# Where the first norm's row vectors live, and where a unit's position row is computed: a two-layer decoder trunk on one core

## The chip, the core and the metric

The kernel runs on one core of a Trainium2 chip (trn2). The metric is the device time of one execution in microseconds (us); the smaller the better. Engines are named as the profile names them: PE is TensorE's matmul, PEld its weight load, DVE is VectorE, ACT is ScalarE, POOL is GpSimd, SP is SyncE, which here issues nearly all DMAs.

## The reference, cut to what matters

Two layers. Each has three token mixers, an output projection with a layer norm, and a mixture of 16 experts with a second layer norm. The change lies in the first norm's last step and in the experts.

```python
def grouped_moe(x, router_w, router_b, w_gate, w_up, w_down):
    ...
    for e in range(N_EXPERTS):
        he = jax.nn.silu(h @ w_gate[e]) * (h @ w_up[e])
        out = out + gate[:, e:e + 1] * (he @ w_down[e])
    ...

for l in range(DEPTH):
    ...
    x = layer_norm(DEEPNORM_ALPHA * x + heads_out @ w_out[l], ln1_g[l], ln1_b[l])
    ffn = grouped_moe(x, router_w, router_b, exp_w_gate[l], exp_w_up[l], exp_w_down[l])
    x = layer_norm(DEEPNORM_ALPHA * x + ffn, ln2_g[l], ln2_b[l])
```

256 tokens of 1,024 values; an expert is 512 wide; every token goes to 2 of 16 experts. The output is the whole `x`, float32.

## The kernel before, in words

**Mixers, then experts, twice.** PE runs through a layer in a written order: projection, mixers, output projection (L1396), transposes of the normalized rows, router, then the experts. Everything from the routing on is in `experts_t` (PE), `experts_s` (ACT) and `experts_v` (DVE), each called through `two_ways`: the engine waits for `v_flag`, loads the word `crowded` and branches. With these inputs the way with `rounds == 1` is taken: one unit of 64 slots for each expert, so 16 units (N = 16).

**Weights.** SP issues all weight loads in one fixed order, 1 MB each: for an expert two halves of gate and of up, then two of down, 6 MB. They go into a ring of 8 + 6 slots (`ring`, `ring_more`) plus two that serve once a layer. A load waits until the last matmul that reads its slot's former content has counted (`last_use`: t_wgu for gate and up, t_wd for down). So 16 MB of a layer's 96 MB of expert weights can be there before the first unit, and from then on a load starts as PE gives a slot back.

**The entry to the experts, in order.** DVE computes the selection, `pick` (a 0/1 matrix that gathers a unit's tokens), the flag and the gates. PE gathers the first four blocks of 128 channels for the first eight experts (`gather`, L427), ACT copies each into `xg` with the norm's gain and shift per channel (L696, s_first), PE runs `first_half` (L518: the first half of expert 0's gate and up), takes the branch, gathers blocks 4 to 7, waits for v_pick, runs `slot_gates(0)` (L532) and two transposes of the positions (L631), and then waits for all eight counts of s_first. Only then comes `hidden(0, 1)` (L552), the second half of expert 0's gate and up. DVE, before its branch, runs `rows_of_x1` (L1581, L1582): `x_tm` times `ln1_g`, plus `ln1_b`, for two tiles of 128 tokens, four operations of 128x1024. The rows of `ln1_g` and `ln1_b`, the same in all 128 partitions, lie in `x_cm`, which is read until the router is done; POOL therefore loads them (two DMAs of 512 KB, L992) only once v_sel has counted. v_pick is given by DVE behind its branch.

**A unit n.** PE: `hidden(n, 1)`, `scatter(n-1)` (L603: y of the unit before, as y_hi + y_lo, added to the tokens' rows in banks 0 to 3 through `pick_t`), `turn(n)` (L567, four transposes of `gu`, waits for v_gu), `position_row(n)` (L611, four matmuls of 32x128 that spread the expert's row of slot numbers), `hidden(n+1, 0)`, `down(n)` (L586). Unit 0 has `hidden(1, 0)` ahead of `turn(0)`. DVE: `take_hidden` (L772: `gu`, the hidden row times the gate), `turned_pick` (L795: `pick_t` from the position row), `product` (L779), `y_low` (L787). ACT: `silu` (L712), `y_high` (L718). The hidden rows of unit n are in bank 4 or 5 (`b_hid[n % 2]`), and the position row overwrites them there once `gu` is taken; `turn` uses bank 6, `down` and the gates bank 7 (`b_y`).

```python
            for n in range(N):
                ...
                if n < N - 1:
                    turn(n)
                    position_row(n)
                ...
                if 0 < n < N - 1 and not turn_of_group:
                    hidden(n + 1, 0)
```

## Time and profile before

| | |
|---|---|
| time, three runs | 864.36, 864.50, 866.28 us; median 864.5 |
| the profiled execution | 866.47 us, its span 864.6 us |
| PE | 800.7 us busy, 93% of the span |
| DVE, ACT, POOL | 315.2 us (36%), 180.6 us (21%), 26.0 us (3%) |
| DMA | 245.87 MB, mean 284 GB/s |
| granted clock of PE, mean | 0.973 |

The time of an execution is a little more than the span from its first to its last instruction. A group of matmuls is given with its start, its length and, in brackets, what PE waited for before it. PE counts as busy also where it runs at half clock. The DMA share is that of the core's 16 DMA engines; it can read slightly over 1.

### The profile page before, as it was taken

Reading aid. Unit: us, or ns where it says so; the run is one execution under the profiler, and the core shown is the slowest. Engines: PE = TensorE matmul, PEld = TensorE weight load, DVE = VectorE, ACT = ScalarE, POOL = GpSimd, SP = SyncE. Lnnn points to the kernel's source line nnn. Section 1 sums busy time; section 2 is a strip of 40 time slices with the busy share of each in tenths; the row PEclk is TensorE's granted clock in tenths of the full one; section 3 lists DMA queues with packets and bytes.
Section 4 is the critical chain, followed back from the end, with each engine's and each line's share of the span. In section 5 each row is a group of like instructions: output and inputs, shape, how many; then the busy total and the mean of one; then the engine's idle time right before and its main releaser. Section 6 shows DMA issues by size and latency. Waiting matters only on the chain. (4 is left out here: it accounts for less than half of the span.)

```text
span 864.6 us, 13075 instructions
## 1 busy us (share of the span) xinstructions
PE 800.7 (93%) x5493; PEld 436.2 (50%) x5493; DVE 315.2 (36%) x646; ACT 180.6 (21%) x371; POOL 26.0 (3%) x103
## 2 busy tenths in 40 slices
PE   9999999988999999989799999999799999999883
PEld 8888666545333333323288876664453333333331
DVE  1296445565111111111343964373741111111115
ACT  1142322333001110000222223232330011100001
POOL 7100000000000000000000000000000000000000
PEclk9999999998999999999989999999999999999998
DMA  9945200397899999999945532014969999999992
GB/s 281 322 150 181 99 2 2 134 425 267 303 417 420 421 421 419 422 422 420 398 143 190 186 108 99 2 68 161 423 255 346 423 420 421 420 421 423 420 421 98
DMA packets 55252, 245.87 MB, mean 284 GB/s; under 512 B 8356, under 2 KB 13328, under 8 KB 30608
## 3 DMA queue, kind: packets, MB, share of 16 engines
q1 hardware_dynamic: 53840, 240.20, 70.3%
q0 software_dynamic: 1344, 4.72, 1.7%
q8 instruction: 48, 0.79, 0.4%
q14 instruction: 20, 0.16, 0.1%
HBM read 243.85 MB, written 1.05 MB: 283 GB/s over the span
## 5 line engine op out<-in xcount | busy, mean ns | idle before, releaser
L552 PE MATMUL bank<-ring,xg 128*64 128x512 f32 x544 | 127.0, 610 | 6.3 <-DMA ring<-in_exp_w_up 3.9
L1054 PE MATMUL bank<-x_cm,ring 128*128 128x256 f32 x576 | 127.8, 383 | 0.9 <-ACT x_cm L2020 0.9
L1054 PEld LDWEIGHTS bank<-x_cm,ring 128*128 128x128 f32 x576 | 110.3, 192 | 17.4 <-ACT x_cm L2020 1.2
L552 PE MATMUL bank<-ring_more,xg 128*64 128x512 f32 x416 | 96.4, 605 | 5.7 <-DMA ring_more<-in_exp_w_up 5.7
L787 DVE TENSOR_TENSOR y_lo<-bank,y_hi 128x512 fp32r<-128x512 f32 x32 | 22.1, 692 | 196.4 <-ACT y_hi L718 187.4
L552 PEld LDWEIGHTS bank<-ring,xg 128*64 128x64 f32 x544 | 38.7, 139 | 76.2 <-issue 74.0
L772 DVE TENSOR_SCALAR x_cm<-bank,g_col 128x512 f32<-128x512 f32 x32 | 24.0, 751 | 107.6 <-PE bank L552 105.1
L552 PEld LDWEIGHTS bank<-ring_more,xg 128*64 128x64 f32 x416 | 30.4, 138 | 58.8 <-issue 57.7
L586 PE MATMUL bank<-ring_more,x_cm 128*64 128x512 f32 x256 | 58.2, 596 | 1.9 <-issue 1.9
L586 PE MATMUL bank<-ring,x_cm 128*64 128x512 f32 x256 | 57.8, 594 | 1.1 <-DVE g_col L763 1.1
L1061 PE MATMUL bank<-ring,x_cm 128*128 128x512 f32 x128 | 57.7, 599 | 0.0
L1396 PE MATMUL bank<-ring,x_cm 128*128 128x512 f32 x128 | 55.6, 592 | 0.0
L718 ACT ACTIVATE y_hi<-bank 128x512 fp32r<-128x512 f32 x32 | 19.1, 597 | 169.8 <-PE bank L586 169.8
L712 ACT ACTIVATE x_cm<-bank 128x256 f32<-128x256 f32 x32 | 12.3, 383 | 179.5 <-PE bank L567 179.5
L1396 PEld LDWEIGHTS bank<-ring,x_cm 128*128 128x128 f32 x128 | 24.0, 190 | 28.7 <-issue 28.7
L1061 PEld LDWEIGHTS bank<-ring,x_cm 128*128 128x128 f32 x128 | 23.7, 190 | 27.3 <-issue 26.8
L586 PEld LDWEIGHTS bank<-ring,x_cm 128*64 128x64 f32 x256 | 18.0, 137 | 35.8 <-issue 34.3
L586 PEld LDWEIGHTS bank<-ring_more,x_cm 128*64 128x64 f32 x256 | 17.9, 137 | 34.0 <-issue 33.3
L696 ACT ACTIVATE xg<-bank,ln_cm 128x512 f32<-128x512 f32 x32 | 23.7, 776 | 46.8 <-PE bank L427 46.1
L567 PE MATMUL bank<-ident,x_cm 128*128 128x128 f32 x128 | 23.9, 309 | 8.6 <-DVE x_cm L772 8.6
L567 PEld LDWEIGHTS bank<-ident,x_cm 128*128 128x128 f32 x128 | 17.9, 209 | 24.1 <-DVE x_cm L772 22.5
L795 DVE TENSOR_SCALAR pick_t<-bank,slot_col 128x128 fp32r<-128x128 f32 x32 | 11.2, 351 | 39.5 <-PE bank L611 37.3
(381 smaller groups left out, 873.9 us busy)
## 6 DMA issues: line engine op xcount, KB each, us to landing
ring<-in_exp_w_gate SPq DMA_DIRECT2D x36, 1024.0 KB, 17.1
ring<-in_exp_w_up SPq DMA_DIRECT2D x36, 1024.0 KB, 18.8
ring_more<-in_exp_w_down SPq DMA_DIRECT2D x32, 1024.0 KB, 18.3
ring<-in_exp_w_down SPq DMA_DIRECT2D x32, 1024.0 KB, 15.4
ring_more<-in_exp_w_gate SPq DMA_DIRECT2D x26, 1024.0 KB, 17.2
ring_more<-in_exp_w_up SPq DMA_DIRECT2D x26, 1024.0 KB, 18.9
ring<-in_w_in SPq DMA_DIRECT2D x24, 1024.0 KB, 8.1
ring<-in_w_out SPq DMA_DIRECT2D x8, 1024.0 KB, 6.3
```

Source lines behind the costliest of these rows:

```text
L552: m = T.matmul(b[half_of(n, i), :], xg[g][:, 4 * h + k, cols], w[:, k, :], start=(h == 0 and k == 0), stop=(h == 1 and k == 3))
L567: m = T.transpose(b_turn[:, tile_(fb)], gu[:, fb::FB], ident[:])
L586: m = T.matmul(b[SL * hf:SL * hf + SL, :], he[n % 2][:, fb, :], w[:, 2 * (fb % 2) + hf, :], start=(fb == 0), stop=(fb == FB - 1))
L696: return A.activation(out_.rearrange("p (u j s) -> p j u s", u=GU, j=TT), in_.rearrange("p (j u s) -> p j u s", u=GU, j=TT), ACT.Identity, ...
L712: mark(A.activation(act_g, b_turn[:].rearrange("p (b a s) -> p b a s", b=FB, a=2)[:, :, side_of(n, 0)], ACT.Silu), "s_silu")
L718: mark(A.activation(y_hi[:], y_bank(n, N)[:], ACT.Copy), "s_yhi")
L772: mark(V.tensor_scalar(gu, b_hid[n % 2][:], g_col[:, n // GU % 2, n % GU:n % GU + 1], None, ALU.mult), "v_gu")
L787: mark(V.tensor_tensor(y_lo[:], y_bank(n, N)[:], y_hi[:].bitcast(F32), ALU.subtract), "v_ylo")
L795: mark(V.tensor_scalar(pick_t[:], b_hid[n % 2][:, 0:P], slot_col[:, r:r + 1], None, ALU.is_equal), "v_pick_t")
L1054: m = T.matmul(out_, w[:, k, c:c + n], x_cm[:, k, :], start=(k == 0), stop=(k == KD - 1))
L1061: m = T.matmul(out_, x_cm[:, k, tile_(j)], w[:, k, c:c + n], start=(k == 0), stop=(k == KD - 1))
L1396: m = T.matmul(bank[4 + 2 * hf + j][:], x_cm[:, b, tile_(j)], w[:, b, :], start=(b == 0), stop=(b == 5))
```

## The change

It does these things:

- `ln1_g` and `ln1_b` get a place of their own, `ln_gain` and `ln_bias`. `ln_bias` shares its place with `y_hi` and `y_lo`. POOL loads them as the layer begins, behind the two loads of the RWKV norm's vectors, and no longer behind v_sel.
- `rows_of_x1` moves on DVE from ahead of the branch to behind `product(0)`. The first `y_high` waits for it (v_x1), as `y_hi` lies where `ln_bias` was.
- PE no longer waits for all of s_first ahead of `hidden(0, 1)`; each of its four pairs of matmuls waits for its own block.
- `position_row(n)` stands ahead of `turn(n)`, and writes into bank 7 (`row_bank`), for all units but the last. The wait for s_pos goes with it, and `turned_pick` reads from there. The wait of gathers for v_pick_t is dropped, and `slot_gates` gets it.

```diff
+        ln_gain = sb("ln_gain", [P, D])
+        with nc.sbuf_tensor("ln_bias", [P, D], F32) as ln_bias:
+            pass
+        y_hi = sb("y_hi", [P, BCOL], F32R)
+        y_lo = sb("y_lo", [P, BCOL], F32R)
...
+        def row_bank(n, N):
+
+            return b_hid[n % 2] if n == N - 1 else b_y
...
                 for k in range(4):
+                    if n == 0 and h == 1 and rounds == 1:
+                        pe.wait_ge(*done("s_first", l, 4 + k + 1))
...
                 pe.wait_ge(*at("v_gu", n + 1))
                 if n:
                     pe.wait_ge(*at("v_he", n))
-                else:
-                    pe.wait_ge(*done("s_pos", l))
...
             def position_row(n):
 
                 e = n // rounds
+                if n == 0:
+                    pe.wait_ge(*at("v_gcol", 2))
+                    pe.wait_ge(*done("s_pos", l))
                 for q in range(P // HS):
-                    m = T.matmul(b_hid[n % 2][HS * q:HS * q + HS, 0:P], ident_b[0:NE, e:e + 1].to_broadcast([NE, HS]),
+                    m = T.matmul(row_bank(n, N)[HS * q:HS * q + HS, 0:P], ident_b[0:NE, e:e + 1].to_broadcast([NE, HS]),
...
-            if rounds == 1:
-                pe.wait_ge(*done("s_first", l))
...
                 if n < N - 1:
+                    position_row(n)
                     turn(n)
-                    position_row(n)
...
-                    pe.wait_ge(*at("v_pick_t", n + 1))
                     mark(gather(k, b_hid[n % 2]), "t_gather")
...
                     pe.wait_ge(*at("v_gcol", 2 * g))
+                    pe.wait_ge(*at("v_pick_t", n + 1))
                     slot_gates(g)
...
                 if n:
                     act.wait_ge(*at("t_scat", n))
+                else:
+                    act.wait_ge(*done("v_x1", l))
                 mark(A.activation(y_hi[:], y_bank(n, N)[:], ACT.Copy), "s_yhi")
...
                     product(n)
+                if n == 0:
+                    for j in range(TT):
+                        rows_of_x1(j)
...
-                        pool.wait_ge(*done("v_sel", l))
-                        for i, name in enumerate(("ln1_g", "ln1_b")):
-                            pool.dma_start(ln_rows[0][:, i, :], t[name][l].partition_broadcast(P)).then_inc(ln_loaded.sem, 16)
...
                     if which == 0:
                         for i, name in enumerate(("rwkv_ln_g", "rwkv_ln_b")):
...
+                        for i, name in enumerate(("ln1_g", "ln1_b")):
+                            pool.dma_start(ln_rows[0][i], t[name][l].partition_broadcast(P)).then_inc(ln_loaded.sem, 16)
...
                 do(V.tensor_tensor(gate[:], gate[:], wide(rms_s[:, :, 0], NE), ALU.mult))
-                for j in range(TT):
-                    rows_of_x1(j)
```

The order of DVE's instructions at the entry to the experts, before (`crowded` is the branch's flag; each name in brackets is a semaphore waited for):

```order
L1986 TENSOR_TENSOR gate<-gate,rms_s 128x32 [waits v_chain]
L1581 TENSOR_TENSOR x_rows<-x_rows,x_cm 128x1024 [waits v_xlo,ln_loaded,t_x,v_chain]
L1582 TENSOR_TENSOR x_rows<-x_rows,x_cm 128x1024 [waits v_chain]
L1581 TENSOR_TENSOR x_rows<-x_rows,x_cm 128x1024 [waits ln_loaded,v_xlo,t_x]
L1582 TENSOR_TENSOR x_rows<-x_rows,x_cm 128x1024 [waits v_chain]
L409 TENSOR_LOAD crowded [waits v_flag]
L409 ISA x2
L415 COMPARE_AND_BRANCH
L762 COPY g_col<-bank 64x4 [waits t_first,t_gcol]
L763 COPY g_col<-bank 64x4
L772 TENSOR_SCALAR x_cm<-bank,g_col 128x512 [waits v_gcol,t_wgu]
```

And with the change:

```order
L2000 TENSOR_TENSOR gate<-gate,rms_s 128x32 [waits v_chain]
L414 TENSOR_LOAD crowded [waits v_flag,v_chain]
L414 ISA x2
L420 COMPARE_AND_BRANCH
L774 COPY g_col<-bank 64x4 [waits t_first,t_gcol]
L775 COPY g_col<-bank 64x4
L784 TENSOR_SCALAR x_cm<-bank,g_col 128x512 [waits v_gcol,t_wgu]
L807 TENSOR_SCALAR pick_t<-bank,slot_col 128x128 [waits t_prow]
L791 TENSOR_TENSOR x_cm<-x_cm,bank 128x256 [waits s_silu]
L1595 TENSOR_TENSOR x_rows<-x_rows,ln_gain 128x1024 [waits ln_loaded,v_xlo,t_x]
L1596 TENSOR_TENSOR x_rows<-x_rows,ln_bias 128x1024 [waits v_chain]
L1595 TENSOR_TENSOR x_rows<-x_rows,ln_gain 128x1024 [waits ln_loaded,v_xlo,t_x]
```

The four operations of the norm and their wait for `ln_loaded` now stand behind the first unit's product (a fourth row like the second follows), ahead of the first `y_lo`.

PE's order in units 0 and 1 before, from `slot_gates(0)` on:

```order
L532 MATMUL bank<-gate,pick 32x2 [waits v_pick]
L552 MATMUL bank<-ring,xg 64x512 [waits slot_full5,slot_full4,s_first]
L552 MATMUL bank<-ring,xg 64x512 x7
...
L567 MATMUL bank<-ident,x_cm 128x128 [waits s_pos,v_gu]
L567 MATMUL bank<-ident,x_cm 128x128 x3
L611 MATMUL bank<-pos_t,ident_b 32x128 x4
...
L603 MATMUL bank<-y_lo,pick_t 128x512 x3
L567 MATMUL bank<-ident,x_cm 128x128 [waits v_he,v_gu]
L567 MATMUL bank<-ident,x_cm 128x128 x3
L611 MATMUL bank<-pos_t,ident_b 32x128 x4
L552 MATMUL bank<-ring_more,xg 64x512 [waits slot_full12,slot_full13,s_xg,v_gu]
```

And with the change:

```order
L541 MATMUL bank<-gate,pick 32x2 [waits v_pick]
L563 MATMUL bank<-ring,xg 64x512 [waits s_first,slot_full5,slot_full4]
L563 MATMUL bank<-ring,xg 64x512
L563 MATMUL bank<-ring,xg 64x512 [waits s_first]
...
L623 MATMUL bank<-pos_t,ident_b 32x128 [waits s_pos,v_gcol]
L623 MATMUL bank<-pos_t,ident_b 32x128 x3
L576 MATMUL bank<-ident,x_cm 128x128 [waits v_gu]
...
L612 MATMUL bank<-y_lo,pick_t 128x512 x3
L623 MATMUL bank<-pos_t,ident_b 32x128 x4
L576 MATMUL bank<-ident,x_cm 128x128 [waits v_he,v_gu]
```

The position row's four matmuls have changed places with the four transposes, and the one wait for s_first has become four.

## Rows read from the trace of the kernel before

**Rows 1.** The page: mean busy share of the DMA engines, in 40 slices.

```profile
DMA  9945200397899999999945532014969999999992
```

**Rows 2.** Busy time by stretch: us, PE, PEld, DVE, ACT, POOL, PEclk, DMA share, GB/s.

```profile
340.00:360.00 20.00, 19.76 (x102) 6.90 (x100) 2.83 (x5) 1.58 (x3) 0.00 (x0) 1.00 1.01 422
```

**Rows 3.** Timeline, layer 0, from the entry to the experts to unit 1's scatter.

```profile
205.95 1.22 DVE L1581 TENSOR_TENSOR x_rows<-x_rows,x_cm 128x1024 f32<-128x1024 f32 x1 [4.50 <-DMA x_cm<-in_ln_b]
206.74 2.78 ACT L696 ACTIVATE xg<-bank,ln_cm 128x512 f32<-128x512 f32 x4 [2.90 <-PE bank L427]
...
209.61 1.22 DVE L1582 TENSOR_TENSOR x_rows<-x_rows,x_cm 128x1024 f32<-128x1024 f32 x1
210.68 0.43 PE L532 MATMUL bank<-gate,pick 128*32 128x2 f32 x32 [2.54 <-DVEq L483]
211.42 5.24 PE L552 MATMUL bank<-ring,xg 128*64 128x512 f32 x16
216.70 0.80 SPq L906 DMA_DIRECT2D ring<-in_exp_w_down  x2
221.36 0.42 DVE L779 TENSOR_TENSOR x_cm<-x_cm,bank 128x256 f32<-128x256 f32 x1
223.85 0.33 SPq L906 DMA_DIRECT2D ring_more<-in_exp_w_gate  x1
...
226.33 0.69 DVE L787 TENSOR_TENSOR y_lo<-bank,y_hi 128x512 fp32r<-128x512 f32 x1 [4.55 <-ACT y_hi L718]
228.90 0.51 PE L603 MATMUL bank<-y_hi,pick_t 32*128 32x512 f32 x4
```

**Rows 4.** Busy time by stretches of 1 us, layer 0; columns as in Rows 2.

```profile
212.00:213.00 1.00, 1.00 (x4) 0.23 (x2) 0.00 (x0) 1.00 (x1) 0.00 (x0) 0.50 0.95 401
...
215.00:216.00 1.00, 1.00 (x6) 0.28 (x4) 0.00 (x0) 0.00 (x0) 0.00 (x0) 1.00 0.00 0
...
223.00:224.00 1.00, 1.00 (x6) 0.35 (x4) 0.00 (x0) 0.00 (x0) 0.00 (x0) 1.00 0.39 156
```

**Rows 5.** Timeline, layer 1, the same place.

```profile
637.89 0.43 PE L532 MATMUL bank<-gate,pick 128*32 128x2 f32 x32 [0.29 <-DVEq L483]
...
639.04 3.65 PE L552 MATMUL bank<-ring,xg 128*64 128x512 f32 x16 [0.39 <-ACT xg L696]
```

**Rows 6.** Timeline, layer 1, PE at a unit's turn.

```profile
762.46 0.41 PE L603 MATMUL bank<-y_lo,pick_t 32*128 32x512 f32 x4
...
763.11 0.75 PE L567 MATMUL bank<-ident,x_cm 128*128 128x128 f32 x4 [0.24 <-DVE x_cm L772]
...
763.78 0.23 PE L611 MATMUL bank<-pos_t,ident_b 16*32 16x128 bf16 x4
...
763.95 2.37 PE L552 MATMUL bank<-ring,xg 128*64 128x512 f32 x10
```

**Rows 7.** Timeline: PE's waits for the last expert weights, layer 0, then layer 1.

```profile
385.26 5.35 PE L552 MATMUL bank<-ring_more,xg 128*64 128x512 f32 x16 [2.43 <-DMA ring_more<-in_exp_w_up]
...
410.11 3.65 PE L552 MATMUL bank<-ring_more,xg 128*64 128x512 f32 x16 [0.89 <-DMA ring_more<-in_exp_w_up]
...
810.27 3.65 PE L552 MATMUL bank<-ring_more,xg 128*64 128x512 f32 x16 [2.41 <-DMA ring_more<-in_exp_w_up]
...
825.18 5.35 PE L552 MATMUL bank<-ring,xg 128*64 128x512 f32 x16 [2.42 <-DMA ring<-in_exp_w_up]
```

**Rows 8.** Timeline and stretch: weight loads at the start of layer 0.

```profile
22.46 32.78 SPq L906 DMA_DIRECT2D ring<-in_w_in  x12
...
37.53 0.84 ACT L2038 ACTIVATE big<-bank,om_mu 128x256 f32<-128x256 f32 x2 [6.07 <-PE bank L1054]
...
30.00:38.00 8.00, 8.00 (x39) 7.04 (x38) 0.87 (x2) 1.31 (x4) 0.00 (x0) 1.00 1.05 343
```

**Rows 9.** The page's DMA issues: KB each, us to landing.

```profile
ring<-in_w_in SPq DMA_DIRECT2D x24, 1024.0 KB, 8.1
```

**Rows 10.** Timeline, layer 1: a long DVE operation of 1,024 elements.

```profile
621.57 1.95 DVE L1599 TENSOR_TENSOR x_lo<-x_rows,x_hi 128x1024 fp32r<-128x1024 f32 x1
```

More of the change, by code:

```diff
@@ L281, in hybrid_trunk @@
         he = [x_cm[:, 3 + i].rearrange("p (b s) -> p b s", b=FB) for i in range(2)]
-        y_hi = sb("y_hi", [P, BCOL], F32R)
-        y_lo = sb("y_lo", [P, BCOL], F32R)
         slot_full = [ctx.enter_context(nc.semaphore(f"slot_full{i}")) for i in range(NSLOT + MORE)]
@@ L1580, in affine_rows @@
                     dve.wait_ge(ln_loaded.sem, 64 * l + 32 * (which + 1))
-                    do(V.tensor_tensor(x_tm[:, j], x_tm[:, j], ln_rows[which][:, 0], ALU.mult))
-                    inc(V.tensor_tensor(x_tm[:, j], x_tm[:, j], ln_rows[which][:, 1], ALU.add), "v_x1" if which == 0 else "v_x2")
+                    do(V.tensor_tensor(x_tm[:, j], x_tm[:, j], ln_rows[which][0], ALU.mult))
+                    inc(V.tensor_tensor(x_tm[:, j], x_tm[:, j], ln_rows[which][1], ALU.add), "v_x1" if which == 0 else "v_x2")
                 def out_half(j, hf):
```

18 lines of the change are left out of this document (9 added, 9 removed).

## The prediction

> **What bounds the kernel now.** I read the page's slices first. The DMA engines are busy to nine tenths or more in two long stretches, slices 12 to 20 and 32 to 39 [rows 1]: the experts of the two layers. The table of busy time by stretch then gives the rate there, 422 GB/s at a share of 1.01 [rows 2]. An expert is 6 loads of 1,024 KB, 6.29 MB, so 14.9 us at that rate. PE also reads as full in that stretch, but it needs less for a unit: the turn at 763.11 [rows 6] follows the one before by 12.3 us, with nothing late. PE lives on the loads made ahead, and at the end of the stage it waits: 2.43 and 0.89 us in layer 0, 2.41 and 2.42 us in layer 1, each time for a DMA [rows 7]. So the experts are a stream of weights, and its end is set by when it starts to flow and by its bytes. A microsecond saved on PE in the middle only lengthens the waits at the end.
>
> What starts the stream is PE giving slots back in the first units. The timeline of layer 0's entry [rows 3] shows how badly that goes. PE stands for 2.54 us until 210.68, since its last gather ended at 208.14, and the releaser is DVE's queue: DVE is still at the four norm operations, the last starting at 209.61, because it had itself stood 4.50 us waiting for the DMA of `ln1_b`, and v_pick is given behind them. After the pause the 16 matmul records of `hidden(0, 1)` take 5.24 us; the same work takes 3.65 us in layer 1 [rows 5]. The stretches tell why: granted clock 0.50 at 212 to 213, so 1.2 GHz, and 1.00, so 2.4 GHz, at 215 to 216 [rows 4]. The next loads are issued at 216.70 [rows 3], right behind that hidden half, and the DMA engines had run dry: share 0.00 at 215 to 216. There is one more gap at 223 to 224, share 0.39 [rows 4], before the next slots come free.
>
> **The change, part by part.** *Norm vectors early, norm operations late (the main term).* DVE no longer stands between the gates and v_pick, so slot_gates can start at 208.14. From slot_gates to `hidden(0, 1)` it is 211.42 - 210.68 = 0.74 us, so the latter starts at 208.88: 2.54 us earlier. ACT's four copies run from 206.74 to 209.52 [rows 3], 0.70 us each, and with the wait split in four they are ready at 207.4, 208.1, 208.8 and 209.5. The pairs, 3.65 / 4 = 0.91 us apart, want them at 208.9, 209.8, 210.7 and 211.6. No wait. With the old single wait it would have been 209.52, so the split alone is worth 0.64 of the 2.54 us. PE now comes without a pause, and in layer 1, where the pauses at the same place are 0.29 and 0.39 us, the half runs at full clock [rows 5]. So I take 5.24 - 3.65 = 1.59 us for the clock. **Layer 0: 2.54 + 1.59 = 4.13 us**, at the end of `hidden(0, 1)`.
>
> *Layer 1.* There the gathers end at 637.89 - 0.29 = 637.60 and the hidden half starts at 639.04 [rows 5]. With 0.76 us for slot_gates and transposes (the 0.43 us record and what follows; 0.74 us in layer 0) it starts at 638.36. **0.68 us.** No clock comes back, it was full.
>
> *Position row ahead of the turn.* In a unit PE ends its scatter at 762.87 and waits 0.24 us for v_gu, turns at 763.11, and the position row shows between the turn and the hidden half: 763.95 - 763.78 = 0.17 us of its own [rows 6]. Ahead of the turn it fits into the 0.24 us, so a unit loses 0.16 us. In unit 0 there is no such wait: `turn(0)` follows `hidden(1, 0)`, and v_gu is long there, so the row delays turn, silu, product and down by 0.16 us, where before it lay under that chain. Which release decides? The engines run dry before the slots of `down(0)` come back, and are nearly full from those of `hidden(1, 1)` and `hidden(2, 0)` on; the first two of these see the 0.16 us loss, the third has it back from unit 1. If the backlog is only solid a unit or two later, each gives 0.16 us more. So the position rows are worth between -0.16 and +0.3 us a layer at the stream's start; I take 0, the value at `hidden(2, 0)`. Behind the last load of layer 1, from 825.18 on, PE sets the end again, and unit 14's row is worth 0.16 us. In layer 0 the last hidden half waits 0.89 us for its load [rows 7], so nothing.
>
> *Does the stream follow?* The two loads issued at about 206.4 last until about 213. The next two can now be issued at 216.70 - 4.13 = 212.6, so these four run on without a gap, until some 5 us later, 218. The next slot, given back in `down(0)`, comes at 223.85 - 4.0 = 219.9 [rows 3]. The engines still run dry for over a microsecond, so PE still sets the start, and the whole 4.13 us goes through.
>
> *The norm operations in their new place.* Four times 1.22 us and the gaps, 4.9 us, behind `product(0)`, which ended at 221.78 [rows 3]. In the old frame of time they end at 226.7; y_hi, which now waits for them, at 227.4; y_lo, 0.69 us [rows 3], at 228.1. PE asks for them at 228.90. Cover left: 0.8 us, given by `down(0)` and `hidden(1, 1)`. The same in layer 1. Cost 0. DVE has nothing else to do there; `take_hidden(1)` comes at 229.07.
>
> *Where the loads go.* 1 MB leaves the entry, where nothing but DVE waited for it. At layer 1's start it is issued at about 442, and the DMA slice there is nearly empty [rows 1]. At layer 0's start it falls at about 27 us into a full stretch: share 1.05, 343 GB/s, at 30 to 38 [rows 8]. 1.05 MB at 343 GB/s is 3.1 us that the projection's loads can be late. The first of them is issued at 22.46 [rows 8] and such a load lands in 8.1 us [rows 9], so at 30.6; PE first reads it when the first four projection steps are done, at 37.5, when ACT takes the last of them up [rows 8]. Cover 7 us, against 3.1. Cost 0, bound 3.1.
>
> *Dropped waits for v_pick_t* (one unit): under the stream, 0.
>
> Sum: 4.13 + 0.68 + 0.16 = 4.97, **5.0 us**. Against the profiled execution that is 866.47 to 861.5. The median of the runs is 864.5, and the same sum gives **859.5 us**.
>
> **The rivals.** *Full clock already (R1).* The runs differ by 2 us, 864.4 and 866.3, and the profile is one of the long ones. Equal pauses did different things: 2.41 us at 810 and the half ran 3.65 us, 2.42 us at 825 and it ran 5.35 us [rows 7]. So in the median run the half behind the 2.54 us pause may have had 2.4 GHz. Then 1.59 us are not there to win: 5.0 - 1.6 = 3.4, **861.1 us**. For it: the rows 7. Against: 2 of those 3 pauses of 2.4 us were followed by half clock, and here PE's pause is longer and followed by 0.74 us of tiny matmuls. The Trainium skill (TensorE: Matmul & The Clock Gate, "Part 1: The HAM clock gate (the 'warmup' mystery)") says that the gate's watching runs freely and does not restart with the kernel, so that one kernel's slow matmuls vary from run to run; by that rule the clock's part is a chance of each run, and the two rows of equal pause agree.
>
> *More than the sum (R2).* The backlog becomes solid a unit or two later (0.3 us a layer), and the half clock at 825 goes as well; of its 1.7 us only some 0.8 us counts, since the next loads land 2.5 us apart and the last hidden half, at 835.8, would meet its load at about 835. Together 1.4: **858.1 us**.
>
> *The start pays (R3).* The whole 3.1 us lands on layer 0's projection: 859.5 + 3.1 = **862.6 us**. For it: the full stretch. Against: PE is busy 8.00 of 8.00 us there [rows 8] and the cover of 7 us. The Trainium skill (DMA: Bandwidth & Descriptors, "Issuing engines are not separate DMA queues") speaks against this part of the change: DMAs of any issuer run on the same 16 engines and interleave, so a second queue buys no room. The trace agrees as to the stretch, whose share is 1.05.
>
> *The stream doesn't follow (R4).* PE starts earlier, and the loads end when they did, because the engines themselves set the end: only 0.16 to 0.7 us remain, **864 us**. Against: the share of 0.00 at 215 [rows 4].
>
> *Slower (R5).* The first y chain takes the place of the wait removed. If the norm operations run longer beside PE and ACT, `scatter(0)` waits. The dearest row of that size is 1.95 us [rows 10] instead of 1.22; four of them add 2.9, less the cover 0.8: PE stands 2.1 us in each layer, and a pause of that size can bring the half clock, 1.7 us more [rows 7]. 2 x 3.8 = 7.6 against 5.0: **867.1 us**. It starts to cost from 0.2 us more an operation. Against: L1581 and L1582 took 1.22 us both with PE busy and idle; the row of 1.95 us writes another type and order.
>
> **How the numbers follow.** Forecast 0.60, R1 0.18, R2 0.08, R3 0.04, R4 0.06, R5 0.04. The measurement can tell 0.3%, 2.6 us, from no change. Faster is then the forecast, R2 and nearly all of R1, 0.85; within 0.3% are R3, R4 and a rest of R1, 0.11; slower R5, 0.04. The range goes from R2 with 0.3 us of scatter, 857.8, to between R1 and R3, 862.2: it holds the forecast, R1 and most of R2.
>
> **What would show it.** In the changed profile: no wait for DVE ahead of slot_gates in either layer; layer 0's hidden half in 3.65 us at clock 1.00; the loads behind it issued about 4.1 us earlier after the gathers; DMA share above 0.9 through what was 213 to 217; `scatter(0)` without a wait; the position rows ahead of each turn and the following hidden half 0.84 - 0.17 us after the turn's start; the waits for the last weights still there, and each later event of the stage about 4 us earlier in layer 0. Wrong would be a wait of y_hi's users, a PE gap before 60 us, or a last load that lands when it did.

## The result, and the profile after

The changed kernel takes **857.37 us**, the median of 10 runs (854.63 to 860.97), beside 864.50 us, the median of 10 runs of the kernel before (861.27 to 866.28). The ratio is 0.9922, with a 95% interval of 0.9903 to 0.994. So it is faster, by 7.1 us, where 5.0 had been forecast and the range began at 857.8. Two further measurements, on other chips, gave 0.9909 (0.9886 to 0.9932) and 0.9925 (0.991 to 0.994).

The profiled execution took 854.63 us, its span 852.9 us. PE is busy for 794.7 us (93%), DVE 316.6, ACT 180.5, POOL 25.9 us; DMA moves the same 245.87 MB at a mean of 288 GB/s; the mean granted clock is 0.979. The slices of the page that answer to [rows 1]:

```profile
DMA  9955200396999999999974522023969999999992
GB/s 285 311 203 194 104 2 2 119 425 256 343 423 420 421 420 421 422 420 422 397 231 153 198 100 101 2 90 153 423 227 375 423 419 422 420 421 422 421 420 99
```

The two stretches at some 422 GB/s are as solid as before. Nothing in them runs faster; they begin earlier.

The timeline of layer 0's entry after, answering to [rows 3] (start, length, engine, line; in brackets how long the engine stood, and what released it). Lines have moved by 5 to 14: L541 is slot_gates, L563 the hidden halves, L595 `down`, L623 the position row, L576 the turn, L612 the scatter:

```profile
204.50 0.39 PE L432 MATMUL bank<-pick,x_hi 128*128 128x256 f32 x1
...
206.40 0.28 PE L432 MATMUL bank<-pick,x_lo 128*128 128x256 f32 x1
206.61 0.43 PE L541 MATMUL bank<-gate,pick 128*32 128x2 f32 x32
...
207.29 3.65 PE L563 MATMUL bank<-ring,xg 128*64 128x512 f32 x16
210.77 3.60 PE L563 MATMUL bank<-xg 128*64 128x512 f32 x16
210.98 0.80 SPq L921 DMA_DIRECT2D ring<-in_exp_w_down  x2
214.30 0.23 PE L623 MATMUL bank<-pos_t,ident_b 16*32 16x128 bf16 x4
214.47 0.75 PE L576 MATMUL bank<-ident,x_cm 128*128 128x128 f32 x4
216.14 1.22 DVE L1595 TENSOR_TENSOR x_rows<-x_rows,ln_gain 128x1024 f32<-128x1024 f32 x1
...
218.29 0.33 SPq L921 DMA_DIRECT2D ring_more<-in_exp_w_gate  x1
219.79 1.23 DVE L1596 TENSOR_TENSOR x_rows<-x_rows,ln_bias 128x1024 f32<-128x1024 f32 x1
221.13 0.60 ACT L730 ACTIVATE y_hi<-bank 128x512 fp32r<-128x512 f32 x1 [5.43 <-DVE x_rows L1596]
221.83 0.69 DVE L799 TENSOR_TENSOR y_lo<-bank,y_hi 128x512 fp32r<-128x512 f32 x1 [0.81 <-ACT y_hi L730]
223.34 0.51 PE L612 MATMUL bank<-y_hi,pick_t 32*128 32x512 f32 x4
223.68 0.41 PE L612 MATMUL bank<-y_lo,pick_t 32*128 32x512 f32 x4
```

PE goes from its last gather (206.68) straight into slot_gates at 206.61, and from there into `hidden(0, 1)` at 207.29, with no wait in brackets. That half takes 3.65 us instead of 5.24. The next two loads are issued at 210.98, 4.30 us behind the last gather's end; before it was 216.70 - 208.14 = 8.56 us [rows 3]. The norm operations run from 216.14 to 221.02 at 1.22 and 1.23 us each. y_hi is done at 221.73 and y_lo at 222.52; the scatter's matmuls of y_hi start at 223.34 and those of y_lo, which alone wait for `v_ylo`, at 223.68.

Table of busy time by stretch, after, answering to [rows 4] (window, length, PE, PEld, DVE, ACT and POOL busy with instruction counts, granted clock, DMA share, GB/s):

```profile
214.00:215.00 1.00, 1.00 (x10) 0.63 (x8) 0.34 (x1) 0.00 (x0) 0.00 (x0) 1.00 0.98 418
...
218.00:219.00 1.00, 1.00 (x8) 0.42 (x6) 1.00 (x2) 0.00 (x0) 0.00 (x0) 1.00 0.00 0
219.00:220.00 1.00, 1.00 (x8) 0.44 (x6) 0.97 (x2) 0.00 (x0) 0.00 (x0) 1.00 0.68 115
```

The first dry gap is gone (share 0.98 behind the turn). One is left: the engines stand again at 218 to 219, because the next slot only comes back in `down(0)`. That gap was in the prediction, as the reason why PE still sets the start; the last experiment takes it up.

The waits for the last weights are still there, answering to [rows 7]:

```profile
378.48 3.65 PE L563 MATMUL bank<-ring_more,xg 128*64 128x512 f32 x16 [2.60 <-DMA ring_more<-in_exp_w_up]
393.38 5.35 PE L563 MATMUL bank<-ring,xg 128*64 128x512 f32 x16 [2.58 <-DMA ring<-in_exp_w_up]
...
783.92 3.65 PE L563 MATMUL bank<-ring,xg 128*64 128x512 f32 x16 [1.68 <-DMA ring<-in_exp_w_up]
798.84 3.65 PE L563 MATMUL bank<-ring_more,xg 128*64 128x512 f32 x16 [2.59 <-DMA ring_more<-in_exp_w_up]
813.76 5.35 PE L563 MATMUL bank<-ring,xg 128*64 128x512 f32 x16 [2.60 <-DMA ring<-in_exp_w_up]
```

Layer 1 waits three times, 6.87 us in all, where [rows 7] have two waits, 4.83 us: PE is earlier than the stream by more than the stream is earlier than before. A part of it is the position rows. From turn to turn a unit late in layer 1 now takes 12.11 us (738.14 to 750.25), where before it took 12.28, and what PE saves in the middle comes back as waiting at the end. Over the experiments below, layer 1's waits for weights add up to 6.3 to 8.1 us in the six profiles that have the row ahead of the turn and the old order of slots, and to 3.7 to 5.1 us in the seven that have it behind.

**A clock of our own for both layers.** To compare executions whose earlier parts differ, I count each layer from the first matmul that reads the selection (L1449 before, L1463 after). The rows of before that this needs:

```profile
198.91 0.19 PE L1449 MATMUL bank<-sel_b,tri_b 128*128 128x32 bf16 x1 [0.15 <-DVE sel_b L1972]
...
626.80 0.19 PE L1449 MATMUL bank<-sel_b,tri_b 128*128 128x32 bf16 x1 [2.20 <-DVE sel_b L1972]
...
629.07 0.41 PE L427 MATMUL bank<-pick,x_lo 128*128 128x256 f32 x1
...
633.40 1.23 DVE L1581 TENSOR_TENSOR x_rows<-x_rows,x_cm 128x1024 f32<-128x1024 f32 x1 [4.07 <-DMA x_cm<-in_ln_b]
...
635.42 0.39 PE L427 MATMUL bank<-pick,x_hi 128*128 128x256 f32 x1
```

and of after:

```profile
617.58 0.19 PE L1463 MATMUL bank<-sel_b,tri_b 128*128 128x32 bf16 x1
...
624.64 0.39 PE L432 MATMUL bank<-pick,x_hi 128*128 128x256 f32 x1
...
627.43 3.65 PE L563 MATMUL bank<-ring,xg 128*64 128x512 f32 x16
```

Beside them stands the stream mark: the moment by which the packets of the hardware queue, counted by their ends, add up to 60 MB (layer 0) and 190 MB (layer 1) since the start. Both lie deep in the solid stretches, so the mark tells how early the stream is.

| from the selection, us | gathers of block 4 | `hidden(0, 1)` | stream mark |
|---|---|---|---|
| before, layer 0 | 7.05 | 12.51 | 74.63 |
| before, layer 1 | 8.62 | 12.24 | 99.43 |
| after, layer 0 | 7.06 | 9.85 | 70.09 |
| after, layer 1 | 7.06 | 9.85 | 97.26 |

The stream is 4.54 us earlier in layer 0 and 2.17 us in layer 1; behind the second mark after takes 0.36 us less. Together 7.07 us. That this is so near the measured 7.1 is partly luck, as the experiments show: these are two single executions, and others of the same kernels have marks up to 2.1 us (before's entry, layer 0) and 1.6 us (changed, layer 1) elsewhere. The two profiled spans themselves lie 11.7 us apart. The other 4.7 us lie where both kernels do the same: 1.47 us ahead of layer 0's selection, and 3.21 us between the first mark and layer 1's selection. The experiments say what they are.

### The profile page after: what moved, and what is told of

Same layout as the page of the kernel before. It is cut to its first block and busy times, and to the rows that moved or that the text cites. A ratio compares the mean times of both kernels' runs of the same rounds, so it can differ in the third digit from the quotient of the medians.

```text
span 852.9 us, 13075 instructions
## 1 busy us (share of the span) xinstructions
PE 794.7 (93%) x5493; PEld 433.2 (51%) x5493; DVE 316.6 (37%) x646; ACT 180.5 (21%) x371; POOL 25.9 (3%) x103
## 2 busy tenths in 40 slices
DMA packets 55252, 245.87 MB, mean 288 GB/s; under 512 B 8356, under 2 KB 13328, under 8 KB 30608
## 5 line engine op out<-in xcount | busy, mean ns | idle before, releaser
L563 PE MATMUL bank<-ring,xg 128*64 128x512 f32 x544 | 127.2, 610 | 10.3 <-DMA ring<-in_exp_w_up 8.3
L1068 PE MATMUL bank<-x_cm,ring 128*128 128x256 f32 x576 | 125.9, 379 | 1.2 <-ACT x_cm L2032 0.9
L563 PE MATMUL bank<-ring_more,xg 128*64 128x512 f32 x416 | 94.6, 596 | 5.2 <-DMA ring_more<-in_exp_w_up 5.2
L563 PEld LDWEIGHTS bank<-ring,xg 128*64 128x64 f32 x544 | 39.0, 139 | 80.7 <-issue 78.5
L595 PE MATMUL bank<-ring_more,x_cm 128*64 128x512 f32 x256 | 58.2, 596 | 3.4 <-issue 3.4
L563 PEld LDWEIGHTS bank<-ring_more,xg 128*64 128x64 f32 x416 | 29.8, 137 | 57.6 <-issue 55.9
L595 PE MATMUL bank<-ring,x_cm 128*64 128x512 f32 x256 | 57.8, 594 | 1.1 <-DVE g_col L775 1.1
L595 PEld LDWEIGHTS bank<-ring_more,x_cm 128*64 128x64 f32 x256 | 18.3, 137 | 35.4 <-issue 34.4
L595 PEld LDWEIGHTS bank<-ring,x_cm 128*64 128x64 f32 x256 | 18.0, 137 | 35.8 <-issue 34.3
L576 PE MATMUL bank<-ident,x_cm 128*128 128x128 f32 x128 | 23.9, 309 | 4.0 <-DVE x_cm L784 1.8
L791 DVE TENSOR_TENSOR x_cm<-x_cm,bank 128x256 f32<-128x256 f32 x32 | 13.5, 421 | 30.1 <-ACT x_cm L722 30.1
```

The lines of the kernel that those rows point to most:

```text
L563: m = T.matmul(b[half_of(n, i), :], xg[g][:, 4 * h + k, cols], w[:, k, :], start=(h == 0 and k == 0), stop=(h == 1 and k == 3))
L576: m = T.transpose(b_turn[:, tile_(fb)], gu[:, fb::FB], ident[:])
L595: m = T.matmul(b[SL * hf:SL * hf + SL, :], he[n % 2][:, fb, :], w[:, 2 * (fb % 2) + hf, :], start=(fb == 0), stop=(fb == FB - 1))
L791: mark(V.tensor_tensor(he[n % 2], act_g, b_turn[:].rearrange("p (b a s) -> p b a s", b=FB, a=2)[:, :, side_of(n, 1)], ALU.mult), "v_he")
L1068: m = T.matmul(out_, w[:, k, c:c + n], x_cm[:, k, :], start=(k == 0), stop=(k == KD - 1))
```

## Experiments

Four kernels each time ran on one chip, and shared the runs of before there. "Hidden" below is the start of `hidden(0, 1)` counted from the selection, "mark" the stream mark, each for layer 0 and layer 1, from the kernel's one profiled execution.

**1. The changed kernel again.** No edit.

> The changed kernel once more, to see how much of the 7.1 us between the medians is the change and how much is scatter of single executions (its spans went from 852.9 to 859.2 us). Theory A (the sum of the prediction holds, 4.1 us at layer 0's entry, 0.7 in layer 1, 0.2 at the end, and the rest is PE's clock falling at other places in one execution than in another): the ratio to the kernel before comes out near 0.994, 859.5 us. Theory B (something of 2 us was left out of the sum): it stays at 0.992, 857.4 us. In the trace both expect PE to run slot_gates without a wait in both layers.

857.27 us (854.61 to 860.14, 6 runs) beside 865.82 (28 runs); ratio 0.9909 (0.9886 to 0.9932). Hidden 9.85 and 9.84, marks 70.10 and 97.53. The result stands, and the time is theory B's: the sum had left something out. A part of it is clock: the changed kernel's runs have a mean granted clock of 0.9777 here, those of before 0.9735. Over the 76 runs of before on the three chips of the experiments, the time falls by some 0.5 us for each 0.001 of mean granted clock (correlation -0.73). So, as an estimate, 2.1 us of this gain go with the clock, and 0.9 us in run 9, where it is 0.9765 beside 0.9746. The prediction had 1.6 us for the clock, in one place.

**2. The norm part alone.** The changed kernel with the single wait for all of s_first, and the position rows as before.

```diff
                 for k in range(4):
-                    if n == 0 and h == 1 and rounds == 1:
-                        pe.wait_ge(*done("s_first", l, 4 + k + 1))
...
             inc(m, "t_pos")
+            if rounds == 1:
+                pe.wait_ge(*done("s_first", l))
...
                 if n < N - 1:
-                    position_row(n)
                     turn(n)
+                    position_row(n)
```

> The norm's part alone: vectors loaded early into their own place, the four operations behind product(0); the single wait for s_first and the old place of the position row are kept. Theory A: layer 0's hidden(0, 1) can start no sooner than ACT's last copy, 0.64 us later than in the changed kernel, and layer 1's keeps its 0.39 us of waiting, less 0.03; so 5.0 - 0.6 - 0.4 - 0.2 (unit 14's row) = 3.8 us under the kernel before, 860.7, give or take 1. Theory B with the missing 2 us in this part: 858.7 or less; with the missing part in the position rows: 860.7 and e3 below the kernel before by 2.

860.70 us (857.54 to 864.46, 11 runs); ratio 0.9946 (0.9928 to 0.9964). Hidden 10.68 and 10.67, marks 70.50 and 97.90. The time is to the digit that of theory A, and that is luck: before took 865.82 us on this chip and not 864.5, so the gain is 5.1 us where theory A had 3.8. This part carries most of the gain, and **in layer 1 its share of the stream is 99.43 - 97.90 = 1.53 us**, more than twice the 0.68 us I had given to everything there.

**3. The position rows alone,** in the kernel before: that part of the diff and nothing else.

```diff
-                    m = T.matmul(b_hid[n % 2][HS * q:HS * q + HS, 0:P], ident_b[0:NE, e:e + 1].to_broadcast([NE, HS]),
+                    m = T.matmul(row_bank(n, N)[HS * q:HS * q + HS, 0:P], ident_b[0:NE, e:e + 1].to_broadcast([NE, HS]),
...
                 if n < N - 1:
-                    turn(n)
                     position_row(n)
+                    turn(n)
```

> The position rows alone, in the kernel before: ahead of the turn, in bank 7. Theory A: -0.2 to +0.5 us of gain, which the times can't tell from the kernel before (864.3); in the trace a unit is 0.16 us shorter on PE, and the weights' stream starts neither sooner nor later than by 0.3 us. Theory B, rows variant: 862.5 or less, and the stream's bytes come 1 us sooner a layer than PE's first unit explains.

864.13 us (859.63 to 867.43, 12 runs); ratio 0.9979 (0.9962 to 0.9997). Hidden 12.25 and 12.19, marks 72.66 and 99.47. In layer 1, where the gathers ran at half clock in both, the mark is that of before, 99.43, so the rows do nothing for the stream's start. In layer 0 it is 1.97 us earlier, though `hidden(0, 1)` starts only 0.26 us earlier: this time the gathers ran at half clock, and the hidden half behind a short pause at full clock:

```profile
209.69 0.43 PE L536 MATMUL bank<-gate,pick 128*32 128x2 f32 x32 [0.66 <-DVEq L483]
...
210.46 3.65 PE L556 MATMUL bank<-ring,xg 128*64 128x512 f32 x16
```

The same entry can thus show either picture. DVE sets the start, 12.2 to 12.5 us after the selection; slow gathers lie under that at little cost, while slow matmuls behind the pause are paid.

**4. The pause kept, PE kept busy in it.** Five short matmuls (ten records) into bank 7, whose result nobody reads, ahead of the wait for v_pick in layer 0; the rest is the kernel before.

```diff
+            if rounds == 1 and l == 0:
+                for i in range(5):
+                    T.matmul(b_y[:, 0:S], ident[:], level_mask[:, 0:4], start=True, stop=True)
             pe.wait_ge(*at("v_pick", 1))
```

> The kernel before, with five matmuls of 128x256 into bank 7, whose result nothing reads, in PE's pause ahead of layer 0's slot_gates (about 2.1 us of the 2.54). It keeps the pause and tells the clock's share apart. If the half clock behind the pause is due to the pause and happens in nearly every execution: hidden(0, 1) runs in 3.65 instead of 5.24 us, 1.6 us less in all, 862.9 us. If the pause brought it only in some executions, as in the rival of full clock: the trace shows 3.65 us as well, but the median is under the kernel before by less than 1 us.

863.08 us (859.45 to 866.18, 12 runs); ratio 0.9968 (0.9953 to 0.9984). Marks 72.80 and 99.54. The timeline:

```profile
207.96 2.32 PE L630 MATMUL bank<-level_mask,ident 128*128 128x256 f32 x10
210.59 0.43 PE L532 MATMUL bank<-gate,pick 128*32 128x2 f32 x32 [0.32 <-DVEq L483]
...
211.27 3.65 PE L552 MATMUL bank<-ring,xg 128*64 128x512 f32 x16
```

`hidden(0, 1)` starts at 12.39, 0.12 us earlier than in before, but takes 3.65 us, and the mark is 1.83 us earlier. But for these 0.12 us, this is the clock's part by itself, forecast at 1.59. The time lies at the 862.9 us of the expectation, which again had taken 864.5 for before: the gain on this chip is 2.7 us. The mark explains 1.8 of them, and the mean granted clock of these runs was 0.9783 beside before's 0.9735, so the low clock was also less elsewhere.

**5. The early load alone.** As 2, and `rows_of_x1` back ahead of the branch.

```diff
                 do(V.tensor_tensor(gate[:], gate[:], wide(rms_s[:, :, 0], NE), ALU.mult))
+                for j in range(TT):
+                    rows_of_x1(j)
...
                     product(n)
-                if n == 0:
-                    for j in range(TT):
-                        rows_of_x1(j)
```

> Only the vectors' early load into a place of their own; the four norm operations stay ahead of DVE's branch, the wait for s_first is single, the position rows are in their old place. Theory A (what PE waited for was the DMA of ln1_b, with the 4.9 us of operations behind it): counted from the matmul that v_sel releases, the gates are ready at 2.4 us, the operations end at 7.4, and PE asks for v_pick at 9.2, so there is no wait for DVE and hidden(0, 1) starts at 10.7 us in both layers, set by ACT's last copy, as in the run of the norm's part alone; 860.7 us against 865.8. Rival (the operations' place matters as much as the load): slot_gates waits for DVE again, start at 11 to 12 us, 863 us.

861.05 us (858.48 to 863.93, 12 runs) beside 864.44 (31 runs); ratio 0.9964 (0.9945 to 0.9983). Hidden 12.25 and 10.67, marks 72.30 and 97.18. That is 3.4 us of gain, where the expectation had 5.1.

```profile
204.41 1.23 DVE L1592 TENSOR_TENSOR x_rows<-x_rows,ln_bias 128x1024 f32<-128x1024 f32 x1
...
208.93 0.43 PE L541 MATMUL bank<-gate,pick 128*32 128x2 f32 x32
...
210.44 3.65 PE L561 MATMUL bank<-ring,xg 128*64 128x512 f32 x16 [0.76 <-ACT xg L705]
```

With the vectors there, DVE is through by 205.64, 3.3 us before PE asks, and no wait for DVE is left. So it was the DMA that made PE wait (4.50 and 4.07 us on DVE), not the place of the 4.9 us of operations. Moving them behind `product(0)` adds nothing here: hidden in layer 1 is 10.67 with them early and 10.67 with them late (experiment 2). The times don't settle it: 0.9964 here and 0.9946 there have intervals that overlap. The move with the vectors still loaded late was not run. (12.25 in layer 0 is again gathers at half clock, this time on the path.)

**6. The split wait alone,** in the kernel before.

```diff
                 for k in range(4):
+                    if n == 0 and h == 1 and rounds == 1:
+                        pe.wait_ge(*done("s_first", l, 4 + k + 1))
...
             inc(m, "t_pos")
-            if rounds == 1:
-                pe.wait_ge(*done("s_first", l))
```

> The kernel before with the wait for s_first split in four, nothing else. Theory A: PE still stands for v_pick, given behind the norm operations some 11.5 us after v_sel, so hidden(0, 1) starts at 12.2 us at the earliest (it was 12.5 and 12.24): 0 in layer 0, 0.3 to 0.4 in layer 1, not to be told from the kernel before (865.8). A start at 11.6 or a time under 864 would say that the split alone carries a part of the gain.

865.17 us (862.16 to 866.93, 12 runs); ratio 1.0007 (0.9986 to 1.0028). Hidden 12.08 and 11.79, marks 73.64 and 100.73. PE waits 2.18 and 1.88 us for DVE, and both halves run slowly behind that:

```profile
208.76 0.43 PE L532 MATMUL bank<-gate,pick 128*32 128x2 f32 x32 [2.18 <-DVEq L483]
...
209.44 5.35 PE L554 MATMUL bank<-ring,xg 128*64 128x512 f32 x16
...
636.12 0.43 PE L532 MATMUL bank<-gate,pick 128*32 128x2 f32 x32 [1.88 <-DVEq L483]
...
636.80 5.35 PE L554 MATMUL bank<-ring,xg 128*64 128x512 f32 x16
```

While DVE is the last to come, the split buys nothing that the time shows. Both starts are 0.4 us earlier than in before. In layer 0 DVE came earlier by itself (slot_gates at 11.40 us from the selection, before 11.77). In layer 1 it did not (11.12 and 11.10), so these 0.45 us are the split's, where 0.3 to 0.4 had been expected; but the mark there is 1.30 us later, as the half behind the pause ran slowly. Note layer 1: its gathers ran at full clock here, and a pause of 1.88 us appears where the profile of before showed 0.29. **That was the hidden size of layer 1's problem.** Run 11, the rows alone a second time, shows it again, with hidden at 12.24 and the mark at 100.83:

```profile
635.47 0.43 PE L536 MATMUL bank<-gate,pick 128*32 128x2 f32 x32 [2.19 <-DVEq L483]
...
636.28 5.16 PE L556 MATMUL bank<-ring,xg 128*64 128x512 f32 x16
```

**7. The changed kernel without the position rows,** the split kept.

```diff
-            return b_hid[n % 2] if n == N - 1 else b_y
+            return b_hid[n % 2]
...
                 if n < N - 1:
-                    position_row(n)
                     turn(n)
+                    position_row(n)
```

> The changed kernel with the position rows back in their old place and bank (the dropped waits restored). Theory A: 0.3 us dearer than the changed kernel at most, start of hidden(0, 1) unchanged at 9.85 us from v_sel, turn(0) 0.16 us sooner: 857.5 against 857.3. If the position rows alone are worth the 1.7 us that their own run measured: 859 us.

859.46 us (856.68 to 861.40, 8 runs); ratio 0.994 (0.9916 to 0.9965). Hidden 9.84 and 9.84, marks 69.73 and 97.27. Against experiment 2 the split brings hidden 0.84 us forward (0.64 forecast) and the marks 0.77 and 0.63 us (0.36 and 0.64 in run 10, the same kernel): once DVE is out of the way the split is worth about what the timeline says. The times are too coarse for it: 0.994 and, in run 10, 0.9937 beside experiment 2's 0.9946.

**8. PE kept busy at the layers' boundary.** The changed kernel with 22 short matmul records behind layer 0's last scatter, against the half clock that shows up there.

```diff
             scatter(N - 1)
+            if l < L - 1:
+                for i in range(11):
+                    T.matmul(b_y[:, 0:S], ident[:], level_mask[:, 0:4], start=True, stop=True)
```

> The changed kernel with eleven matmuls of 128x256 into bank 7, whose result nothing reads, behind the last scatter of layer 0, where PE stands 5.6 us for the norm and then runs at half clock (10.2 us of it in the kernel before, 6.8 in the changed one). If the pause is what brings the half clock there: no half clock between the last scatter and 15 us into layer 1, the transposes of the rows take 2.0 instead of 3.7 us and the first projection runs at full clock, 2 to 3.5 us under the changed kernel: 854 to 855.5. If the matmuls hold PE longer than the pause, some of it is lost.

859.72 us (858.93 to 861.82, 12 runs); ratio 0.9946 (0.9929 to 0.9962), no gain over the changed kernel, where 854 to 855.5 us had been expected. Hidden 9.84 in both layers, marks 69.65 and 96.76. The filler ends, PE stands, and the next transposes come 7.5 us behind the stage's end instead of 5.5:

```profile
424.04 5.02 PE L703 MATMUL bank<-level_mask,ident 128*128 128x256 f32 x22
431.63 3.31 PE L1045 MATMUL bank<-ident,x_rows 128*128 128x128 f32 x16 [2.58 <-issue]
```

In its profile the granted clock is 1.00 until 432, through the filler and the pause, and then 0.53 at 432 to 435: the low stretch comes later and is shorter than in the profile after, but the transposes are 2 us late. The norm behind the last scatter was no later than before (it begins 0.05 us behind the scatter's end here and 0.06 in after), so PE didn't stand for it. The profile has one thing that moved with the transposes, a packet of 16 KB in the queue of instructions, here at 429.01:

```profile
q8 instruction: 1, 0.02, 34.5%
```

(the DMA view of 428.9 to 429.1: packets, MB, share). In the other thirteen profiles such a packet starts 2.87 to 3.00 us behind the scatter's end, here 4.90 us, as the filler ends. In all fourteen the transposes begin 2.59 to 2.63 us behind its start. So the likely cause is that PE waits at the boundary for its next instructions, and the filler puts off their loading. No run here changes that alone, so it is not shown.

**9 to 11. What the position rows are worth.** The times of 1, 3 and 7 gave them some 2 us, the traces only 0.3. So the changed kernel, the changed kernel without the rows, and the rows alone ran together on one chip.

> The changed kernel again, as the other side of the next run on the same chip. Ratio to before 0.9865 to 0.994 by the two measurements so far (0.9922 and 0.9909); the position rows are worth what separates it from the next run: 0 to 0.4 us if they are worth what the trace shows (nothing where the stream starts, 0.3 us at a layer's end), 2 to 2.5 us if the times of the first measurements hold.

> The changed kernel with the position rows as before, a second time. Theory A (a unit without the row's stall is 0.16 us shorter, only the last units of a layer show it): within 0.5 us of the changed kernel. Theory B (the rows are worth 2 us and more over the whole): slower than the changed kernel by 1.5 to 3 us, as 859.46 against 857.27 was.

> The kernel before with the position rows alone, a second time. Theory A: ratio to before 0.9990 to 1.0005. Theory B: 0.9965 to 0.9985, as the 0.9979 of the first time.

| | median, us (runs) | ratio to before (865.57 us, 17 runs) |
|---|---|---|
| changed kernel | 858.89 (6) | 0.9925 (0.991 to 0.994) |
| without the rows | 859.97 (6) | 0.9937 (0.9918 to 0.9956) |
| rows alone | 864.75 (12) | 0.9994 (0.9978 to 1.001) |

The rows alone land on theory A: hidden 12.64 and 12.24, marks 72.50 and 100.83, the latter beside the 100.73 of experiment 6, which also had its gathers at full clock and has no rows. Most of their first 0.9979 goes with the mean granted clock: there it was 0.9762 on average beside 0.9735 for before, by the slope of experiment 1 some 1.4 of the 1.7 us; here it was 0.9746 for both. In the changed kernel 1.1 us separates the medians, between the theories and less than the scatter of either side (3.7 and 4.8 us from the shortest run to the longest). All four comparisons lean the same way, by 0.8 to 2.2 us, two of them with a higher clock on the side with the rows or across chips. So more than the trace's 0.3 us is not shown, and up to some 2 us not excluded.

Run 9 also tells what the 4.7 us are. It is the changed kernel, and its span is 859.0 us, 6.1 us over the profile after:

```profile
422.00:429.00 7.00, 3.60 (x16) 3.28 (x16) 5.32 (x13) 5.01 (x13) 0.00 (x0) 0.53 1.06 386
429.00:430.00 1.00, 0.28 (x1) 0.30 (x2) 1.00 (x3) 0.34 (x1) 0.00 (x0) 1.00 1.01 367
```

is the layers' boundary in the profile after (granted clock 0.53, then 1.00), and in run 9:

```profile
426.00:436.00 10.00, 7.94 (x26) 6.76 (x27) 8.32 (x15) 3.73 (x10) 0.00 (x0) 0.50 0.98 335
...
624.00:626.00 2.00, 2.00 (x12) 2.00 (x11) 0.77 (x5) 0.99 (x2) 0.00 (x0) 0.50 0.15 61
```

From the first mark to layer 1's selection it takes 353.23 us, where after took 350.05 and before 353.26. Its layer 1 gathers ran at half clock, hidden came at 11.36 and the mark at 98.86, only 0.57 us ahead of before's. So one kernel's executions differ by 6 us, and where they differ the low clock falls differently. One execution of the changed kernel has the 3.2 us and another has not, and the old entry shows both as well (experiment 3 takes 350.04 us over the same stretch). So the 4.7 us need not be the change. Whether the change makes the short picture more frequent can't be told from one profile a kernel.

**12. The two once-a-layer slots two pairs of loads later.** In the changed kernel `hidden(1, 0)` reads its weights from the two slots that serve once a layer (the matmuls with `xg` alone as source at 210.77), so it gives nothing back to the ring. With one line changed they take the loads 8 and 9 of a layer instead of 4 and 5.

```diff
-            cycle = aged[:4] + [NSLOT + MORE + i for i in range(ONCE)] + [NSLOT + i for i in range(MORE)] + aged[4:]
+            cycle = aged[:4] + [NSLOT + i for i in range(4)] + [NSLOT + MORE + i for i in range(ONCE)] + [NSLOT + i for i in range(4, MORE)] + aged[4:]
```

> The changed kernel with one line of the slots' order changed: the two slots that are used once a layer take the loads 8 and 9 of a layer instead of 4 and 5, so that the slots of hidden(1,0) come to the next loads ahead of those of down(0). If DMA waits for a slot given back between the first three pairs of loads and the down product (share 0.00 in the us before down(0) ends), that gap closes and the whole stream is earlier by its length, 1 to 3 us a layer: 853 to 856 us, and the 60th MB behind v_sel at 67 to 69.5 us instead of 70.1. Rival: the order of slots only shifts the gap to later loads, the stream is as before, time within 0.5 us of the changed kernel.

**854.80 us** (852.34 to 856.46, 5 runs); ratio 0.9876 (0.9859 to 0.9894), on the same chip as run 9's 0.9925. That is within the 853 to 856 us expected, and the rival, no more than 0.5 us from the changed kernel, falls. Marks 68.93 and 97.42, the latter with gathers at half clock; run 9 in that state had 98.86. The last dry gap in run 9:

```profile
219.00:220.00 1.00, 1.00 (x8) 0.49 (x6) 1.00 (x2) 0.00 (x0) 0.00 (x0) 1.00 0.18 66
220.00:221.00 1.00, 1.00 (x7) 0.35 (x5) 1.00 (x1) 0.00 (x0) 0.00 (x0) 1.00 0.61 115
```

and in run 12, where the loads are issued right behind `hidden(1, 0)`:

```profile
219.00:220.00 1.00, 1.00 (x8) 0.41 (x6) 1.00 (x2) 0.00 (x0) 0.00 (x0) 1.00 1.01 426
220.00:221.00 1.00, 1.00 (x8) 0.45 (x6) 0.97 (x2) 0.00 (x0) 0.00 (x0) 1.00 0.98 418
...
215.44 0.33 SPq L921 DMA_DIRECT2D ring_more<-in_exp_w_gate  x1
215.81 0.43 SPq L921 DMA_DIRECT2D ring_more<-in_exp_w_up  x1
```

From the release at 215.44 on the share is 0.95 or more in each us to 227. The marks are 1.4 us earlier in each layer than run 9's, and the medians 4.1 us apart; between them lie a shorter end of each stage (1.1 and 0.4 us from mark to last scatter and to the end, by the profiles) and the scatter of 5 and 6 runs. It beats both kernels.

## Why the prediction was right or wrong

**Direction and mechanism: right.** The stretches of loads set the time, their start is set by PE's early slots, and the gain is how much earlier those come. It was named, and the marks show it in both layers.

**Layer 0's pause and clock, 4.13 us: right for the execution it was read from.** 4.54 measured at the mark. The loads behind `hidden(0, 1)` are issued 4.26 us earlier after the gathers (8.56 to 4.30). The clock's part was 1.59 by the rows and 1.83 in experiment 4. R1, in which the hidden half already has the full clock, is nonetheless real. Of the four profiles with before's entry in layer 0 (before and runs 3, 6 and 11) the half ran slowly in two, marks 74.63 and 73.64, and at full clock in two, marks 72.66 and 72.50. Against the last two the change wins 2.6 and 2.4 us in layer 0. In both the gathers had been slow and the pause was short (0.66 and 1.15 us), so it was not quite R1's picture, a full clock behind the long pause, but it has R1's price.

**Layer 1, 0.68 us: wrong, and this is the step that failed.** I took the two waits in the row, 0.29 and 0.39 us, as what DVE cost. But they were short only because PE was late itself: its gathers before had run at half clock (0.41 us a record at 629.07 against 0.28 in layer 0, and 8.62 against 7.05 us to block 4). DVE held slot_gates at 11.10 us from the selection, and ACT's last copy, late as the gathers were, put `hidden(0, 1)` at 12.24. With DVE gone it starts at 9.85, 2.39 us earlier, if the gathers have their clock; the mark moves 2.17 us. If they haven't, as in run 9, it starts at 11.36 and the mark moves 0.57 us, close to what I had forecast. And where the old entry had fast gathers (runs 6 and 11), PE stood 1.88 and 2.19 us, the half behind ran slowly, and the marks are 100.73 and 100.83: against those the changed kernel's 97.26 and 97.53 are 3.2 to 3.6 us earlier. So "No clock comes back" held only where the gathers had been slow. I had summed over a wait where I should have compared two chains: DVE's, from the selection to v_pick, and PE's at its full clock.

**Position rows, 0 at the stream's start and 0.16 us at the end: right by the trace,** not settled beyond. The mark of layer 1 is 99.47 with them and 99.43 without (slow gathers), 100.83 with and 100.73 without (fast ones). In the unit they do what was forecast: the row at 224.01, the turn at 224.32, the hidden half at 225.00, 0.68 us behind the turn, where 0.67 had been worked out.

**Split wait, 0.64 of the 2.54 us: right in kind,** 0.84 once DVE is gone, and nothing (1.0007) while DVE is there. It belonged in the sum only behind the other edit.

**Norm operations late, 0: right,** and with more cover than forecast. The 0.8 us were counted from y_lo's end to the matmuls of y_hi, and by that count it is 223.34 - 222.52 = 0.82. But the code waits for y_lo only ahead of its own matmuls, so the cover is 223.68 - 222.52 = 1.16 us. R5 (slower operations there) did not occur: 1.22 and 1.23 us. What it would cost beyond the cover wasn't tried. The move itself was not needed for the gain (experiment 5).

**Loads at the layer's start, 0 with a bound of 3.1: right within the scatter.** The selection of layer 0 comes at 197.44, 196.95 and 198.78 us in the three profiles of the changed kernel. Over all nine profiles in which the vectors are loaded early the mean is 198.64, with one at 201.49 (experiment 8, with 10.2 us of half clock from 135 on); over the five in which they are loaded late it is 198.32 (197.36 to 198.91). R3's 3.1 us falls. So does R4: the end of `hidden(0, 1)` comes 4.25 and 2.39 us earlier from the selection, and the marks moved by 4.54 and 2.17.

**The sum.** By the pair of profiles 4.54 + 2.17 + 0.36 = 7.07 us, beside 4.13 + 0.68 + 0.16 = 4.97. The missing 2.1 us are layer 1's 1.5, and 0.6 of small terms. In run 9 the same three differences are 4.30, 0.57 and 0.67, 5.5 us, while the medians beside it lie 6.7 us apart. So the failed step is the term of layer 1, by 1.5 us in the pair of profiles; how the 7.1 us of the medians divide over the layers and the low clock elsewhere is not shown to better than some 2 us. R2 named the right side and the right size (858.1) for other reasons: a backlog solid later, which the marks bound at 0.4 us, and a half clock at the end, which is still there (5.35 us at 813.76).

## What to carry to other kernels

A short wait does not say that the other engine costs little: look at what the waiting engine did before it, and whether it came late by itself; then compare both chains from their last common event, at full clock. Where a stream of loads sets the time, follow the DMA share in the first microseconds after it may start, and put the slots that come free first under the loads that come next; slots that serve only once belong to loads whose release nobody waits for. A vector load that is issued only when its place becomes free can hold a whole entry; a place of its own, 4 KB per partition for each vector, ended that here.

## What the runs showed of the hardware

Low clock falls into different places in executions of one program, and its place counts beside its amount. In the 28 runs of before on one chip the mean granted clock goes from 0.971 to 0.977 and the time from 862.86 to 868.36 us; the two go together only loosely there (correlation -0.52; -0.82 and -0.74 on the two other chips). In a gather under DVE's chain it costs little (hidden at 12.2 to 12.6 with it, in before and runs 3 and 11, at 12.51 and 12.24 without). Behind the pause it costs 1.8 us (experiment 4). At the layers' boundary its length goes with 2 to 3 us: from the end of layer 0's last scatter to layer 1's selection it is 197.9 to 198.9 us in the four profiles with 3.4 or 6.8 us of half clock there (after with 6.8), and 200.4 to 201.0 in the nine with 10.2 us (before, run 9); run 8, with its late transposes, is left out. The Trainium skill (TensorE: Matmul & The Clock Gate, "Part 1: The HAM clock gate (the 'warmup' mystery)") says that the gate's watching runs freely, so that one kernel's slow matmuls vary from run to run; the traces of these executions agree (layer 1's gathers took 0.28 us a record in the profile after and 0.41 in run 9). For reading profiles that means: a difference of 6 us between two single executions of this kernel is no finding, while differences counted from a common event, in the same clock, repeat to some 0.3 to 0.4 us (marks 70.09, 70.10 and 70.33 in the three profiles of the changed kernel; 69.73 and 70.14 in the two without the rows).

Filler matmuls were followed by the full clock where they ended 0.3 us before the real work could start (experiment 4), and by the low one where PE stood 2.58 us behind them (experiment 8). That stand moved with a 16 KB packet of the instruction queue: in all fourteen profiles PE's first transposes of layer 1 begin 2.59 to 2.63 us behind it.
